# Delta scan of a two-block transformer kernel: one filler product moved between the masks of two tiles, one moved ahead of the block products, two weight loads on another queue, GpSimd's squares ordered behind VectorE's

## The reference

```
def gated_delta_chunked(q, k, v, g, beta, s0):
    ...
    decay = jnp.exp(jnp.where(incl, g[..., :, None] - g[..., None, :], -jnp.inf))
    kb = k * beta[..., None]
    m = jnp.where(strict, jnp.einsum('bhnid,bhnjd->bhnij', kb, k) * decay, 0.0)
    a = m + jnp.eye(c, dtype=F32)
    ...
    sol = lax.linalg.triangular_solve(a, rhs, left_side=True, lower=True, unit_diagonal=True)
    u, w = sol[..., :dv], sol[..., dv:]
    attn = jnp.einsum('bhnid,bhnjd->bhnij', q, k) * decay
    ...
    def step(s, xs_n):
        v_new = u_n - jnp.einsum('bhck,bhkv->bhcv', w_n, s)
        o_n = jnp.einsum('bhck,bhkv->bhcv', qg_n, s) + jnp.einsum('bhij,bhjv->bhiv', attn_n, v_new)
        s = s * gl_n[..., None, None] + jnp.einsum('bhck,bhcv->bhkv', kd_n, v_new)
        return s, o_n
```

## Time and profile before

| what | value |
|---|---|
| median of 3 executions | 2011.09 us (2010.02 to 2011.14) |
| the profiled execution | 2010.3 us |
| its span, first to last instruction | 2008.5 us |
| mean granted TensorE clock, share of full | 0.984 |
| busy: TensorE, VectorE, ScalarE, GpSimd | 92%, 33%, 20%, 3% |
| delta scan on TensorE's timeline | about 206.8 to 435.5 us |

### The profile page before, as it was taken

How to read it: one execution, slowest core, us unless ns; L and a number is a source line. 1 busy time by engine, 2 the same in 40 slices (tenths; PEclk the granted TensorE clock), 3 DMA queues, 4 the chain that set the end, 5 groups by cost and what they waited for, 6 DMA issues and landing times.

```text
span 2008.5 us, 23773 instructions
## 1 busy us (share of the span) xinstructions
PE 1854.2 (92%) x9223; PEld 1026.6 (51%) x9223; DVE 668.6 (33%) x1443; ACT 407.5 (20%) x824; POOL 67.5 (3%) x103
## 2 busy tenths in 40 slices
PE   6999999999999899998888998888899799999997
PEld 3447457887887443333323333332333255777775
DVE  1888566347622211221210212121121214432223
ACT  3223620436221110111100101110010023511011
POOL 1000500100000000000000000000000000000000
PEclk9999998999999899999999999999999999999999
DMA  9714457325474899999999999999999942124442
GB/s 389 280 63 159 145 147 182 109 87 152 130 279 200 332 428 427 428 428 429 428 429 429 428 429 428 429 428 428 428 429 427 404 170 97 63 84 157 156 157 94
DMA packets 98579, 568.36 MB, mean 283 GB/s; under 512 B 33104, under 2 KB 43216, under 8 KB 67408
## 3 DMA queue, kind: packets, MB, share of 16 engines
q1 hardware_dynamic: 92192, 561.93, 69.8%
q10 hardware_dynamic: 6320, 5.51, 0.9%
HBM read 555.55 MB, written 11.67 MB: 282 GB/s over the span
## 4 chain that ended last, share of the span: by engine, by line
PE 40%; DMA 20%; DVE 3%; issue 3%; ACT 1%; DVEq 0%; SPq 0%
PE close_bank L2294 11%; DMA expert_ring<-in_w_gu_units 10%; DMA tail<-in_w_gu_units 9%; PE close_bank L2659 7%; PE close_bank L2240 6%; PE close_bank L2669 4%; PE close_bank L2212 3%; PE close_bank L2486 3%; PE close_bank L2596 1%; DVE ob L2122 1%; PE close_bank L2581 1%; DVE oa L2102 1%; PE close_bank L2650 1%; PE close_bank L2281 0%; DVE hT L2130 0%
## 5 line engine op out<-in xcount | busy, mean ns | idle before, releaser
L2240 PE MATMUL close_bank<-expert_ring,hT 128*64 128x512 f32 x1536 | 342.7, 595 | 44.5 <-DMA expert_ring<-in_w_gu_units 44.5
L2240 PEld LDWEIGHTS close_bank<-expert_ring,hT 128*64 128x64 f32 x1536 | 106.0, 137 | 265.0 <-issue 182.4
L2129 DVE TENSOR_SCALAR hT<-close_bank 128x512 f32<-128x512 f32 x32 | 22.1, 692 | 465.1 <-PE close_bank L2240 465.1
L2294 PE MATMUL close_bank<-expert_ring,h2T 128*64 128x512 f32 x384 | 167.4, 592 | 0.0
L2294 PE MATMUL close_bank<-expert_ring,hT 128*64 128x512 f32 x384 | 167.4, 592 | 0.0
L2183 ACT ACTIVATE hT<-hT 128x512 f32<-128x512 f32 x32 | 20.1, 629 | 699.7 <-DVE hT L2129 699.7
L499 PE MATMUL mix_in_pj<-hT,mix_in_pj_ring 128*128 128x512 f32 (+1 forms) x384 | 140.8, 527 | 3.0 <-DVE hT L631 2.7
L2659 PE MATMUL close_bank<-hT,expert_ring 128*128 128x256 f32 x640 | 141.4, 379 | 0.0
L2659 PEld LDWEIGHTS close_bank<-hT,expert_ring 128*128 128x128 f32 x640 | 121.6, 190 | 25.1 <-issue 9.6
L153 PE MATMUL delta_scan_fill_bank<-hT,fill_w 128*128 128x512 f32 (+1 forms) x320 | 112.4, 510 | 5.4 <-PEq L80 2.8
L499 PEld LDWEIGHTS mix_in_pj<-hT,mix_in_pj_ring 128*128 128x128 f32 x384 | 73.0, 191 | 68.4 <-issue 62.7
(11 more groups left out here) (488 smaller groups left out, 2426.9 us busy)
## 6 DMA issues: line engine op xcount, KB each, us to landing
expert_ring<-in_w_gu_units SPq DMA_DIRECT2D x96, 2048.0 KB, 29.1
expert_ring<-in_w_down_units SPq DMA_DIRECT2D x48, 2048.0 KB, 32.3
tail<-in_w_gu_units SPq DMA_DIRECT2D x16, 2048.0 KB, 30.5
late<-in_w_gu_units SPq DMA_DIRECT2D x16, 2048.0 KB, 29.1
mix_in_wm<-in_w_mod_units SPq DMA_DIRECT2D x11, 2048.0 KB, 12.8
expert_ring<-in_w_up_units SPq DMA_DIRECT2D x22, 1024.0 KB, 5.7
fill_w<-in_w_fill SPq DMA_DIRECT2D x38, 512.0 KB, 4.1
late<-in_w_down_units SPq DMA_DIRECT2D x8, 2048.0 KB, 34.5
```

Source lines behind the costliest of these rows:

```text
L2129: v.tensor_scalar(glu, gb[j], LIMIT, None, ALU.min).then_inc(s_glu, 1)
L2240: m = pe.matmul(b[halves[h], :], xT[:, k, x], unit[z][:, r0 + c0 + 512 * h:r0 + c0 + 512 * h + 512], start=False, stop=(k == KT - 1))
L2294: m = pe.matmul(yb[h][halves[j], :], hidT[j][:, c, hh * SLOTS:(hh + 1) * SLOTS], unit[z][:, r0:r0 + 512], start=False, stop=(f == 7))
```

## The change

Filler 6 is multiplied between the third and the fourth tile's products (TensorE: `fill(t + 4)` for t = 1 and 2), and copied behind the fourth tile's decay (ScalarE: `copy_fill(t + 3)` for t = 2 and 3), ahead of the k copies. Filler 18 joins the run before the block products, every later one moves up a place, so that fillers 22 and 23 are left behind "d6". The loads of fillers 18 and 19 go from SyncE's queue to ScalarE's, behind the copies of fillers 14 and 15. GpSimd's squares of q wait for VectorE's squares of k. SyncE's loop with store_m, load_m and the stores of fillers 0 to 9 is as before.

```
@@ -906,18 +906,17 @@
                     sp.wait_ge(s_xs[d], 32)
                     for b in TLB[d][0:2]:
                         low(sp, d, b, s_x1[d])
-                S.fill.load(sp, 18)
                 for d in d2:
                     for b in TTB[d][0:2]:
                         diagonal(sp, d, b, s_x2[d])
-                S.fill.load(sp, 19)
+                S.fill.load(sp, 20)
                 for d in d2:
                     low(sp, d, TLB[d][2], s_x3[d])
                     for b in TTB[d][2:]:
                         diagonal(sp, d, b, s_x3[d])
-                for f in (18, 19):
-                    S.fill.load(sp, f + 2)
-                    S.fill.store(sp, f)
+                S.fill.store(sp, 18)
+                S.fill.load(sp, 21)
+                S.fill.store(sp, 19)
                 for d in d2:
                     copied(sp, ("y6", d, NTILE - 1))
                     sp.dma_start(qg[d].rearrange("p t h n -> p (t h n)"),
@@ -959,8 +958,8 @@
                 act.activation(egl[:], egl[:], ACT.Exp).then_inc(s_eg, 1)
                 for t in range(1, NTILE):
                     decay(t)
-                    if t == 2:
-                        copy_fill(5)
+                    if t >= 2:
+                        copy_fill(t + 3)
                 for t in range(NTILE):
                     if t == 2:
                         store_m(act, 1)
@@ -968,15 +967,18 @@
                         see(act, ("k", t, g))
                         act.activation(ktok[:, t, heads[g]], bank[TURN["k", t, g][0]][:], ACT.Copy).then_inc(freesem(("k", t, g)), 1)
                 load_m(act, 1)
-                for f in range(6, 18):
+                for f in range(7, 18):
                     if f in (8, 9):
                         S.fill.load(act, f + 8)
                     if 10 <= f < 14:
                         S.fill.load(act, f + 2)
                     copy_fill(f)
+                    if f >= 14 and f < 16:
+                        S.fill.load(act, f + 4)
                     if f >= 10:
                         S.fill.store(act, f)
                 copy_fill(18)
+                copy_fill(19)
                 for c in range(2):
                     for d in d2:
                         f, x = PAIRS[d][0]
@@ -984,17 +986,17 @@
                         act.activation(tl[d][:].rearrange("p t h n -> p (t h) n")[quad(x), 16 * c:16 * c + 16, LC[d, f]:LC[d, f] + BLK],
                                        flat(TURN["e5", d, c][0])[quad(x)].rearrange("p (a n) -> p a n", n=BLK),
                                        ACT.Copy).then_inc(freesem(("e5", d, c)), 1)
-                copy_fill(19)
+                copy_fill(20)
                 for t in range(NTILE):
                     see(act, ("y6", 0, t))
                     act.activation(y6s[0][SECOND[0], t], flat(TURN["y6", 0, t][0])[SECOND[0]]
                                    .rearrange("p (h n) -> p h n", h=HA), ACT.Copy).then_inc(freesem(("y6", 0, t)), 1)
-                copy_fill(20)
+                copy_fill(21)
                 for t in range(NTILE):
                     see(act, ("d6", 1, t))
                     act.activation(tt[1][FIRST[1], t, :, SECOND[1]], flat(TURN["d6", 1, t][0])[FIRST[1]]
                                    .rearrange("p (h n) -> p h n", h=HA), ACT.Copy).then_inc(freesem(("d6", 1, t)), 1)
-                for f in range(21, F1):
+                for f in range(22, F1):
                     copy_fill(f)
                 for n in range(NTILE):
                     for i, (d, g) in enumerate(BATCH):
@@ -1020,6 +1022,7 @@
 
                 g.memset(xx[0], 0.0)
                 g.memset(xx[1], 0.0).then_inc(s_x0, 1)
+                g.wait_ge(s_sqk, HA // HALF)
                 g.tensor_tensor(sqq, q[:], q[:], ALU.mult).then_inc(s_sqq, 1)
                 g.wait_ge(s_x0, 1)
                 for d in d2:
@@ -1190,12 +1193,12 @@
                                 right = k[:, hh, t * P:(t + 1) * P] if kind == "kg" else q[:, hh, (t - 2) * P:(t - 1) * P]
                                 m = pe.matmul(b[:, h, :], k[:, hh, t * P:(t + 1) * P], right, start=True, stop=True)
                             m.then_inc(fullsem((kind, t, g)), 1)
-                    if t == 1:
-                        fill(5)
+                    if t in (1, 2):
+                        fill(t + 4)
                 for t in range(NTILE):
                     for g in g2:
                         turn("k", k, t, g)
-                for f in range(6, 18):
+                for f in range(7, 19):
                     fill(f)
 
                 pe.wait_ge(s_z, 1)
@@ -1210,7 +1213,7 @@
                                               tt[d][quad(f), t, h, quad(x)], tl[d][quad(f), t, h, LC[d, f]:LC[d, f] + BLK],
                                               start=True, stop=True)
                         m.then_inc(fullsem(("y5", d, c)), 1)
-                fill(18)
+                fill(19)
                 for d in d2:
                     pe.wait_ge(s_x2[d], 32)
                     for c in range(2):
@@ -1234,7 +1237,7 @@
                                                 tt[d][quad(x), t, h, quad(x)], y5s[d][quad(x), a, :], start=True, stop=True)
                     for d in d2:
                         last[d].then_inc(fullsem(("e5", d, c)), 1)
-                fill(19)
+                fill(20)
                 for d in d2:
                     pe.wait_ge(s_x3[d], 48)
                     copied(pe, ("e5", d, 1))
@@ -1247,7 +1250,7 @@
                                                 tt[d][FIRST[d], t, h, SECOND[d]], tl[d][FIRST[d], t, h, :], start=True, stop=True)
                     for d in d2:
                         last[d].then_inc(fullsem(("y6", d, t)), 1)
-                fill(20)
+                fill(21)
                 for d in d2:
                     copied(pe, ("d5", d, 1))
                 for t in range(NTILE):
```

## The result

The changed kernel is slower: 2024.85 us median of four executions against 2011.12 us, ratio 1.0065, 95% interval 1.0052 to 1.0077, so 10.5 to 15.5 us. The profiled execution has a span of 2025.1 us against 2008.5. Of these 16.6 us, 2.4 lie ahead of the stage: filler 2 starts at 209.24 and not at 206.83. That start moved between 206.2 and 212.2 us over all profiled executions, with edits that can't reach it, so it is spread. From filler 2 to the scan TensorE takes 192.82 us (402.06 - 209.24) against 178.66 (385.49 - 206.83): the change costs 14.16 us there, and after it nothing is lost or won. In what follows, times inside the stage are counted from filler 2, since spread outside the stage doesn't enter them.

A forecast was written before the change was run, and what follows sets the result against it. TensorE was 92% busy, and delta-scan delays were taken to reach the end undiminished. Substitution lateness 13.2 to 20.6, less 4.27, less 0 to 1.0, gave +7.9 to +16.3; middle +12.1 on 2010.3: 2022.4 us, range 2016 to 2028.

The forecast's parts named there:

- The copy of filler 6, held by a store two entries down another queue: ScalarE's copy waits for filler 4's store, behind store_m(0) and load_m(0) on SyncE's queue; release at 280.37 to 285.15 us.
- The masks 5.42 us late: VectorE's masks of the fourth tile end at 271.80 us instead of 266.38, since filler 6 delays the products.
- TensorE, filler 7 6.9 to 11.7 us late, block products reached at +12.2 to +17.0: TensorE's delay behind the copy's wait, with slow restart (1.76 us) and filler 18 (3.58 us) added before the block products.
- This chain decides, and I shift all that follows by its 13.2 to 20.6: Masks, block transfers and VectorE's substitution run 13.2 to 20.6 us late and set when the second direction's block products start.
- the 1.71 us: TensorE's gap before the second direction's block products in the kernel before, taken as a wait for that direction's blocks.
- has no slack there: Claim that the substitution's chain was already late at the block products in the kernel before, by that 1.71 us gap.
- The end, -4.27: One narrow filler fewer after the last triangle product: 3.58 us, plus its 0.69 us load wait, saved before the scan.
- Part four at 0: GpSimd's q squares behind VectorE's k squares: both shifts covered by over 3 us, so no effect.
- Part three at 0 to -1.0: Loads 18 and 19 on ScalarE's queue: a 1.03 us gap in filler 18 may go or stay.
- the short bound: Block transfers at their shortest landings, if four stores alone get all DMA engines; the total then lies near 2018 us.

The follow-up runs named there:

- e1: Changed kernel with the store of filler 4 ahead of store_m(0) in SyncE's list: 2016.54 us, ratio 1.0026 to the kernel before.
- e2: Changed kernel with filler 6 still multiplied between the tiles but its copy back behind the k copies and ScalarE's block transfers: ratio 1.0043 to the kernel before.
- e7: Changed kernel with five memsets, each waited for, ahead of the substitution on VectorE to delay it: ratio 1.0072 to the kernel before.
- e5: Changed kernel with the store of filler 4, load of filler 8 and store of filler 5 ahead of store_m(0): ratio 1.0011 to the kernel before.
- e6: e5 with the load of filler 22 also put ahead of the triangle-copy wait and the decay-row loads: ratio 0.9992 to the kernel before.
- e9: Changed kernel run once more with no edit: ratio 1.0066 to the kernel before.
- e11: Changed kernel with filler 6 and its copy back at their old places, and load 22 early: 2008.89 us, ratio 0.9992 to the kernel before.
- e10: Kernel before with only GpSimd's squares of q made to wait for VectorE's squares of k: ratio 1.0003 to the kernel before.
- e8: Changed kernel with the loads of fillers 18 and 19 back on SyncE's queue: ratio 1.0053 to the kernel before.
- e3: Kernel before with only filler 6 and its copy moved up: ratio 1.0048 to the kernel before.
- e4: Changed kernel with filler 6 and its copy back at their old places, the rest of the change kept: ratio 1.0017 to the kernel before.

## Why the prediction was right, and where it was not

The forecast was 2022.4 us, 2016 to 2028, slower with 0.92; measured 2024.85. The sum was +12.1 us, the stage shows +14.16.

- **The copy of filler 6, held by a store two entries down another queue: right.** Predicted release at 280.4 to 285.15; counted as before it is 282.1. e1 and e2 take the wait away, each in its own way.
- **The masks 5.42 us late:** 5.35.
- **TensorE, filler 7 6.9 to 11.7 us late, block products reached at +12.2 to +17.0:** 9.44 and 15.57.
- **"This chain decides, and I shift all that follows by its 13.2 to 20.6": wrong.** The substitution was 8.8 us late and decided nothing; e7 shows its slack. Counted as before, it started at 291.35, where 296 to 303 was forecast. Two readings failed. I took the 1.71 us in the second half of the block products for a wait for its blocks. In the trace of the kernel before, all four transfers of these blocks, issued from 324.60 to 328.29, had landed by 331.94, 4.1 us before the products at 336.07, and the first direction's 2.0 us before its own first product. That the chain "has no slack there" was wrong from the start (the two rows stand below this list). And I put ScalarE's block store behind its k copies, as in the list: its queue issued it at 284.69, while the copy of filler 6 was still running. Since the stores of the two queues no longer ran beside each other, store to load took 5.36 us on SyncE and not 8.18 (in e1, where they run beside each other again, it takes 8.21), and ScalarE's load landed in 3.4 us, half of the 6.84 I used. The sum came out because TensorE's own delay, 15.57 us at the block products and 14.6 at "d5" (155.12 against 140.52), lies near the middle of what I gave the chain. That is luck: the path that I added up isn't the one that decided. Only where TensorE is made punctual, in e5 and e6, does the chain decide, by 1.27 and 0.32 us.
- **The end, -4.27: mis-sized.** It measured -2.58 in the first profile, and in e9 the stretch from "d6" to the scan was even 0.37 us longer than before. The last narrow filler went, but the 0.69 us wait didn't: as 1.76 and 3.02 us it came back at filler 22, whose load now goes out behind the decay rows (at 386.41) and took 7.8 us to land. e6 and e11 remove it.
- **Part four at 0: right** (e10). **Part three at 0 to -1.0:** open, see e8 and e9.
- **The rule of the Trainium skill** (page "Trainium Kernel Development and Optimization", section Key Constraints: two issuing queues share the same DMA engines) pointed to the short bounds for the block transfers, and the runs agree: four block stores alone had landed 5.36 us after the first was issued, with four more beside them 8.18.

The view of line 877 in the kernel before, from 324.5 to 328.8 us, for the reading of the 1.71 us:

```profile
L877 SPq DMA_DIRECT2D delta_scan_tl<-block_t x4: 302/462/1432, 324.6 to 328.3; - x4
DMA to landing us min/median/max: 2.8/4.1/5.1
```

## What to carry to other kernels

When an instruction is moved up on one engine, follow each semaphore it waits for to the queue entry that raises it, and read what stands ahead of that entry: here a copy moved up by a few instructions waited for a store that sat behind two block transfers, which in turn held everything behind the copy. A work item that fills a gap is worth the gap only if what ends the gap isn't delayed by it; otherwise the wait moves on. And of two parallel chains with little between them, find the deciding one by delaying one on purpose before a forecast is hung on it. A gap that the profile puts down to "issue" has to be held against the landing of the data: here one of them (e5) was a wait for data, and the one in the earlier trace rows wasn't.

## What the runs showed of the hardware

**Gaps that no data explain.** In the short products TensorE stops for 0.2 to 3.6 us with "issue" as the only reason. From the changed kernel's timeline, 253 matmul rows and as many weight loads lie between the gap at 357.52 and the next (2.57 us), 127 between that and the third (0.82 us); in the kernel before, 127 between the last two. These places go with the count of instructions and not with the data. In the kernels with filler 18 behind the block products (before, e3, e10) the first gap comes after 129 of them; where its 16 matmuls are ahead, it comes after 241 and in e4 after 113 too, 16 earlier than 129. The page lists instruction fetches as 46 packets with 0.75 MB, 16 KB each, and in the thirteen profiles all 43 of these gaps ended 1.2 to 2.0 us after such a packet had passed; the two at the first block product in e5 and e6 ended instead 0.1 us after the landing of the blocks. The one packet near the gap before 370.56, which passed from 368.17 to 369.13 (the changed kernel, DMA queues from 368.1 to 369.2 us):

```profile
q8 instruction: 1, 0.02, 5.5%
```

The gaps come with idle DMA engines too: the kernel before, its busy times from 352 to 353 us (TensorE, weight load, VectorE, ScalarE, GpSimd, granted clock, DMA share, GB/s), and the row after:

```profile
352.00:353.00 1.00, 0.00 (x0) 0.00 (x0) 0.80 (x2) 0.00 (x0) 0.00 (x0) 1.00 0.00 0
```

```profile
353.19 0.37 PE L1222 MATMUL delta_scan_bank<-delta_scan_tt,delta_scan_r 32*32 32x32 f32 x12 [1.95 <-issue]
```

So the next block of instructions seems to be fetched too late for products of some 15 ns each. The counts and the packets speak for it; no run changed the fetch, and what fills the time from the packet to the restart is open.

**Short waits cost twice.** Behind 2.65 us of waiting in two pieces (2.11 and 0.54), 20 transposes took 4.07 us and not 2.40 (e1), and from 271.80 to 276.90 us the clock was granted at 0.67. The kernel before waited 3.62 us in three pieces (1.28, 1.80, 0.54), and its clock stayed at the full 2.4 GHz from 260.24 to 268.67. From 60 to 80 us after filler 2 the clock was granted at 0.64 in the changed kernel, between its two levels of 1.2 and 2.4 GHz, and at the full 2.4 before (one row of busy times each, the changed kernel first, columns as above):

```profile
269.24:289.24 20.00, 8.32 (x43) 6.41 (x42) 6.70 (x10) 3.80 (x8) 0.00 (x0) 0.64 0.54 127
```

```profile
266.83:286.83 20.00, 20.00 (x62) 9.96 (x61) 5.76 (x24) 3.86 (x7) 0.00 (x0) 1.00 0.85 203
```

**A queue runs ahead of its engine.** ScalarE's block store was issued at 284.69 us, 0.19 us after the copy of filler 6 had begun and before the first of the four k copies (284.99) that stand ahead of the store in the list.
